# A fused two-block forward pass on one core: stage transfers move ahead of the weights' refill on SP, and a batch's inputs are requested two slots sooner

## The reference

```
def layer_ab(x, ...):                     # layer 0
    h = rms_norm(x, norm_g); q, k, v, ... = split(h @ w_in)
    o = concat(gla_chunked(...), forgetting_attention(...))    # GLA 4 heads, FOX 8 heads
    return x + (o * silu(gate)) @ w_out

def layer_c(x, ...):                      # layer 1
    u, gate = split(rms_norm(x, norm_g) @ w_in, 2)
    z = gelu(s5_ssm(u, lam_re, lam_im, log_step, b_re, b_im, c_re, c_im, d))
    z = z * sigmoid(z @ glu_w + glu_b)
    return x + (z * silu(gate)) @ w_out

def s5_ssm(u, ...):    # 128 groups of 16 channels, each with a 64-dim complex diagonal state
    # x_t = Lbar x_{t-1} + Bbar u_t ; y_t = Re(C x_t) + D u_t

# second block, layers 2 and 3
def layer(x, ...):
    h = rmsnorm(x, norm_w) @ w_in
    y = concat(ssd_branch(...), conformer_branch(...), diff_attention_branch(...))
    return x + y @ w_out
```

## Time and profile before

| | |
|---|---|
| median of 3 runs | 3752.86 us (3752.4 to 3756.08) |
| profiled execution, first to last instruction (span) | 3750.1 us |
| PE busy / DVE / ACT / POOL, share of the span | 93% / 57% / 34% / 4% |
| mean granted clock of PE | 0.969 |
| HBM traffic, mean | 152 GB/s |

### The profile page before, as it was taken

The page is one execution under the profiler, slowest core; times in us unless marked ns, Lnnn a source line. Parts: engine busy times, 40 slices in busy tenths (PEclk is TensorE's granted clock), DMA queues, the critical chain, the costliest instruction groups (busy, mean ns, idle before and its releaser), DMA issues.

```text
span 3750.1 us, 42960 instructions
## 1 busy us (share of the span) xinstructions
PE 3497.4 (93%) x15890; PEld 2794.8 (75%) x15890; DVE 2123.9 (57%) x3122; ACT 1288.5 (34%) x2013; POOL 150.3 (4%) x100
## 2 busy tenths in 40 slices
PE   7899998888789999999999999898999999999899
PEld 6687886666667888878877877676777887677677
DVE  6655546465555555543343675566765376556674
ACT  4233334334333223333243224423433222432442
POOL 2000000000001000000031000000002000000000
PEclk9899999999899999999999999999999999999899
DMA  4233334455465555655443443344446343334445
GB/s 152 96 124 119 125 110 164 146 173 194 162 225 184 182 178 178 202 179 191 160 166 113 136 156 112 108 135 148 153 141 235 120 157 133 106 114 151 146 161 193
DMA packets 286130, 574.58 MB, mean 153 GB/s; under 512 B 61393, under 2 KB 101089, under 8 KB 285409
## 3 DMA queue, kind: packets, MB, share of 16 engines
q1 hardware_dynamic: 285920, 571.83, 46.4%
HBM read 440.65 MB, written 131.07 MB: 152 GB/s over the span
## 4 chain that ended last, share of the span: by engine, by line
PE 43%; issue 23%; DVE 15%; ACT 7%; DMA 6%; DVEq 3%; POOLq 1%; SPq 1%; ACTq 0%
PE bank L542 28%; PE bank L541 10%; DVE weights_low L467 3%; DMA arena<-in_s_bc 2%; ACT weights_high L394 2%; DVE arena L1958 2%; DVEq L2536 1%; POOLq L453 1%; ACT arena L1900 1%; DVE residual_in L2032 1%; DMA convert_in<-x 1%; DVE arena L1953 1%; DVE act_low L525 1%; PE bank L1071 1%; DVE arena L1821 1%
## 5 line engine op out<-in xcount | busy, mean ns | idle before, releaser
L542 PE MATMUL bank<-act_high,weights_high 128*128 128x512 f32 x3584 | 1459.3, 407 | 99.2 <-DVE stream_out L514 44.5
L542 PE MATMUL bank<-act_low,weights_high 128*128 128x512 f32 x3584 | 1425.4, 398 | 0.0
L467 DVE TENSOR_TENSOR weights_low<-weights_raw,weights_high 128x1024 fp32r<-128x1024 f32 x528 | 655.4, 1241 | 1094.3 <-ACT weights_high L394 1091.6
L394 ACT ACTIVATE weights_high<-weights_raw 128x1024 fp32r<-128x1024 f32 x528 | 557.8, 1057 | 1523.6 <-PE bank L542 1249.9
L542 PE MATMUL bank<-act_high,weights_low 128*128 128x512 f32 x3584 | 963.7, 389 | 0.0
L542 PEld LDWEIGHTS bank<-act_high,weights_high 128*128 128x128 f32 x3584 | 693.2, 193 | 269.8 <-issue 67.3
L542 PEld LDWEIGHTS bank<-act_low,weights_high 128*128 128x128 f32 x3584 | 692.2, 193 | 140.8 <-issue 2.9
L542 PEld LDWEIGHTS bank<-act_high,weights_low 128*128 128x128 f32 x3584 | 673.1, 188 | 140.6
L541 PE MATMUL bank<-weights_high,act_high 128*128 128x512 f32 x640 | 257.5, 402 | 28.6 <-DVE stream_out L480 23.5
L541 PE MATMUL bank<-weights_high,act_low 128*128 128x512 f32 x640 | 252.6, 395 | 0.0
L2032 DVE SCALAR_TENSOR_TENSOR residual_in<-residual_in,arena 128x512 f32<-128x512 f32 x240 | 180.4, 751 | 20.8 <-issue 1.7
(11 more groups left out here) (318 smaller groups left out, 2966.1 us busy)
## 6 DMA issues: line engine op xcount, KB each, us to landing
weights_raw<-in_w_all SPq DMA_DIRECT2D x528, 512.0 KB, 3.4
convert_in<-mix SPq DMA_DIRECT2D x80, 256.0 KB, 4.0
fm_b<-stream_out SPq DMA_DIRECT2D x72, 256.0 KB, 2.4
mix<-arena SPq DMA_DIRECT2D x64, 256.0 KB, 4.4
x_part<-stream_out SPq DMA_DIRECT2D x48, 256.0 KB, 2.4
residual_in<-x_part SPq DMA_DIRECT2D x12, 1024.0 KB, 6.8
x<-stream_out SPq DMA_DIRECT2D x48, 256.0 KB, 2.4
convert_in<-x SPq DMA_DIRECT2D x48, 256.0 KB, 3.9
```

The source lines that it names most:

```text
L394: e.activation(WH[:, t % 3, :], RAW[:, t % 3, :], ACT.Copy).then_inc(wh_ready, 1)
L467: e.tensor_tensor(WL[:, t % 3, :], RAW[:, t % 3, :], WH[:, t % 3, :].bitcast(F32), ALU.subtract).then_inc(wl_ready, 1)
L542: return e.matmul(bank[s][:, :], a[:, s * P:(s + 1) * P], h, start=start, stop=stop)
```

## The change

It has three parts.
1. In SP's loop `take(t)` moves from the end of the body to right behind `store_sp`, ahead of the refill, the residual load and the conversions.
2. In `sw_sp` the inputs of batch b + 1 are requested in the third slot of batch b, behind a wait for "cp" of batch b. Only batch 0 still requests its own in its first slot. The stores of k and of the sines move to a new fifth slot of each batch (`free[3 * b:3 * b + 5]`, the second slot of the next batch); the generators of DVE, ACT and PE get an empty fifth piece.
3. In `ssd_conv_sp` the store of the result moves from the second to the third slot.

```
         def sw_sp(e, b):
-            if b:
-                e.wait_ge(*sw_d.at("cp", b - 1))
-            else:
+            if b == 0:
                 for x in GLA_DONE:
                     e.wait_ge(*x)
-            e.dma_start(sw_bc, I["s5_bc"][b]).then_inc(sw_in, 16)
+                e.dma_start(sw_bc, I["s5_bc"][b]).then_inc(sw_in, 16)
             yield
             yield
+            if b + 1 < KT:
+                e.wait_ge(*sw_d.at("cp", b))
+                e.dma_start(sw_bc, I["s5_bc"][b + 1]).then_inc(sw_in, 16)
             yield
             e.wait_ge(*sw_a.at("vt", b))
             e.dma_start(WV[b], two_d(sw_vt)).then_inc(sw_vst, 16)
             e.wait_ge(*sw_d.at("cp", b))
             e.dma_start(WC[b], sw_cp[:, :, S5_C:]).then_inc(sw_cst, 16)
+            yield
             e.wait_ge(*sw_d.at("k", b))
             e.dma_start(WK[b], sw_k[0:S5_C]).then_inc(sw_kst, 16)
...
         def ssd_conv_sp(e, l, i):
...
             yield
+            yield
             if i < 8:
                 e.wait_ge(*sd_ca.at("silu", t))
                 e.dma_start(XD[l][i], sd_ring[:, i % 2, :]).then_inc(sd_xst[i % 2], 16)
-            yield
             yield
             yield
...
-            stage(f"s5w{b}", free[3 * b:3 * b + 4], sp=lambda e, b=b: sw_sp(e, b), pe=lambda e, b=b: sw_pe(e, b),
+            stage(f"s5w{b}", free[3 * b:3 * b + 5], sp=lambda e, b=b: sw_sp(e, b), pe=lambda e, b=b: sw_pe(e, b),
...
             for t in range(NU):
                 if t - 1 in ENDS:
                     store_sp(e, ENDS[t - 1])
+                take(t)
                 if t + 5 < NU:
                     weights_sp(e, t + 5)
                 if UNITS[t][0] in XR_TURN and FIRST[UNITS[t][0]] == t:
                     residual_sp(e, UNITS[t][0])
                 for n in BY_SLOT.get(t + 1, ()):
                     convert_sp(e, n)
-                take(t)
```

## The result

The changed kernel takes 3628.01 us, median of 4 runs (3624.53 to 3633.06), against 3754.47 us (3752.4 to 3757.32) for the kernel before, run beside it on the same chip: ratio 0.9664, 95% interval 0.9648 to 0.968. That is 126 us saved.

A forecast was written before the change was run, and what follows sets the result against it. TensorE is 93% busy, so its idle and low-clock time, mostly in the S5 stretch, can be won: 83.6 idle + 21 clock + 5 start - 15 left = 94.6 us, so 3658 us, range 3632 to 3703.

The forecast's parts named there:

- the S5 request: S5 weight batches: requesting inputs right behind their last read removes DVE's 135.6 us wait and most of PE's idle time.
- The first rival: S5 stretch: only PE's direct waits go, its waits for evacuations and exponentials stay; 3703 us, chance 0.14.
- The clock: S5 stretch: of 43.1 us of full-speed work missing at the lower clock, about half costs time; 21 us saved.
- What stays: S5 stretch: idle time and low clock that remain after the change, as in neighbour stretches; 15 us subtracted.
- the stages ahead of the refill, outside the S5 stretch: Small weights' load at the start goes out earlier: 5 us saved, bounds 0 and 9; SSD convolutions' loads counted as nothing.
- from 1500 us on the lengths stay within 3 us: Sign that the forecast is right: stretches of the program after 1500 us keep their length.
- an edit at no cost: Moved k, sines and SSD stores, reordered conversions and residual loads: hidden or unchanged; the fifth step's drains 0.8 us.
- The starved refill: SP held at a stage's wait delays the refill 5 us at 28 places; 3798 us, chance 0.03.
- Growing landings: S5 inputs: closer-packed transfers land 2 us later than the slowest, 12 us reaching PE; 3670 us, chance 0.05.
- The fast bound: Fastest sum, with the whole missing clock, 9 at the start and 6 left: 130 us saved, 3623; range cut at 3632.

The follow-up runs named there:

- the S5 part alone: Kernel before with S5 inputs requested in the third slot of the previous batch and two stores in a fifth slot, nothing else: 3654.7 us, ratio 0.9744.
- run 272: No follow-up kernel: the 272nd time DVE runs line 467, once for each unit in every kernel; its start marks the same program point in two profiles.
- the best version: Changed kernel with S5's weight stages and FOX heads 1 to 7 behind the conversions and the refill last in SP's body: 0.9634 of the kernel before.

## Why the prediction came out 32 us short

**What bounds the kernel, and the S5 request: right.** The wait for `in_s_bc` is gone (forecast: under 15 us), the stretch takes 442.5 us (440 to 455) at a clock of 0.99 (0.97 or more), and PE waits neither for line 918 nor for FOX 0. With the S5 part alone the stretch gains 95.0 of 96.0 us. The first rival, that PE's waits for evacuations had a cause of their own, would have left 3703 and is out: they went with DVE's.

**The clock: right.** The stretch lost 83.6 - 9.0 = 74.6 us of idle time and 96.0 in length, so 21.4 us are clock, where the sum had 21. The missing clock fell from 43.1 to 442.5 x 0.01 = 4.4 us; of the 38.7 us of missing clock that went, 55% had cost time. The Trainium skill's charge of half of all throttled time ("TensorE: Matmul & The Clock Gate", section "HAM oscillation — how this bites in real kernels") is all of these 38.7 us, 1.8 times the measured term.

**What stays: 6 us too careful.** 15 us were left in the stretch for idle time and clock. 9.0 us of idle time stayed, 2.0%, the low end of what the neighbours suggested.

**The step that failed: the stages ahead of the refill, outside the S5 stretch.** "I take 5 us for this" covered the start alone; the stretches outside S5 gained 30.4. With the 6 us above and 0.4 of clock that is the whole miss: 25.4 + 6 + 0.4 = 31.8. The sign that "from 1500 us on the lengths stay within 3 us" failed with it: from run 272 on 17.5 us were gained. Of the 25.4 us the small weights' 9.6 and the SSD store's 4.2 rest on experiments; the rest stands in the profiles alone, and for 4 at the start and 3.3 in the S5 layer the cause stays open.
- The small weights are loaded three times. The prediction costed the first from the earlier trace rows and left out slots 273 and 401, though both are in the code's list and the list of waits names ACT's wait for `in_w_small` as one sum, 23.3 us in 3 pieces (shown below the list). By stretch they brought 8.1 and 1.5 us, shown by putting them back and by moving them alone. At the start the load is worth the 5 us taken; the stretch gained 9.1, all of the bound.
- The SSD convolutions were counted as nothing, because "none of PE's waits names them". PE's wait was there, named after an evacuation of DVE. They gained 6.6 us, of a bound of 8; 4.2 of them hang on the moved store.
- That store was said to "stay where it was", an edit at no cost. It stays where it was only because of this move; without it, the load behind it is late and 4.2 of the 6.6 us in these stretches are lost.
- 3.3 us between runs 138 and 272 stood in both profiles of the changed kernel (3.3 and 3.5), but in those of its variants anything from -0.3 to 4.6; they are not explained.

The wait for the small weights before, from the list of waits, whole span:

```profile
ACT small_weights L689 <- DMA residual_in<-in_w_small: 23.3, 3, 9.1
```

**A cost that was called none.** "Conversions and residual loads now stand behind the stages", with no slot in which a stage waits in its own slot and a conversion stands behind. In slots 110 to 138 they do come late: the changed kernel gains 4.7 us less there than the S5 part alone, and 14 more would be lost without the fifth slot, which the prediction had listed among the edits at no cost as well. The prediction looked for waits on results of the *same* slot alone. With all stores in the fourth slot, those of k and of the sines are such waits. In the changed kernel waits for work begun one slot sooner hold SP too, in this stretch 24.5 us at four FOX stores and 18.4 us at the new request itself:

```profile
SPq L881 <- DVE arena L926: 18.4, 4, 5.5
```

And it did not count that a load which goes out behind the stages' stores also lands later.

**The other rivals.** The starved refill (3798) was given 0.03 and is excluded by holding every refill a whole slot. Growing landings (3670) did not come for the request that the rival was about; they came, unpriced, for the conversions' loads (3.8 to 5.1 us). The tile view of `in_s_bc` after, against 3.1/4.8/6.0 before:

```profile
DMA to landing us min/median/max: 2.6/3.0/4.7
```

The stretch moves 200 GB/s instead of 165 and the landing is shorter. What was requested just ahead goes with it: the median is 4.8 us before, 3.6 with the stages ahead of the refill but the four stores still right ahead of the request, 4.2 with the S5 part alone, where each request follows a refill by less than 3 us, and 3.0 in the changed kernel. The first two differ with the same stores ahead, so this is not the whole of it. In 6 of its 16 requests nothing had gone out for 3 us, and these land in 2.7 us.

**The fast bound.** The prediction had worked out 3623 as its fastest sum and cut it to 3632. Keeping it would have been luck: it reaches 130 us with 43 of clock, where 21 came, and with 9 outside the stretch, where 30 came.

## What to carry to other kernels

On a queue that one engine issues in program order, order the requests of a loop body by how soon each is read, not by size or habit: here the 512 KB refill had 8 us to spare and stood ahead of loads that had none, and the best version puts it last. The costliest thing ahead of a load was here a store that waits for a result of its own slot; what it costs appears three engines later under another name, so when an engine off the path waits for a transfer, follow that wait forward before counting it as nothing. And when an edit moves a class of work, price every place of that class: here one of three loads was costed. Not tried was a second engine that issues transfers, which would take the stores out of this queue altogether.

## What the runs showed of the hardware that was not expected

- More traffic did not lengthen the landing of every transfer: 200 GB/s against 165 in the stretch, with the median landing of the 256 KB inputs down from 4.8 to 3.0 us, while that of the conversions' loads rose from 3.8 to 5.1. What stood in the queue just ahead went with both: 2.7 us with nothing requested for 3 us, 4.2 behind a refill, 8.1 at most behind two stores and a refill. The Trainium skill ("DMA: Bandwidth & Descriptors", section "Queues, rings and completion order") has each DMA engine consume a queue's descriptors in order, and this agrees.
- The time that the low clock cost was close to half of the missing clock at two sizes: 4.16 of 8.55 us around two single waits, 21.4 of 38.7 us over the stretch.
- Runs of one kernel on one chip differ by up to 13 us here (3737.57 to 3750.60 for the kernel before with its small loads ahead), more than several of these edits are worth. The mean granted clock goes with it: 0.971 in the fastest of these runs and 0.966 in the slowest. The lengths of the stretches, within 1 us in the one kernel that was profiled twice and within some 3 us between kernels, could place gains that the medians could not.
